# Eight feed-forward sublayers take the residual turned before its norm

## The reference

```python
def rmsnorm_2(x, w):
    xf = x.astype(jnp.float32)
    y = xf * lax.rsqrt(jnp.mean(xf * xf, axis=-1, keepdims=True) + NORM_EPS)
    return (y * w.astype(jnp.float32)).astype(x.dtype)

def swiglu_2(x, w_in, w_out):
    g, u = jnp.split(x @ w_in, 2, axis=-1)
    return (jax.nn.silu(g) * u) @ w_out

for i in range(DEPTH_2):
    h = h + 0.5 * rmsnorm_2(swiglu_2(rmsnorm_2(h, gn[0]), ffn1_w_in[i], ffn1_w_out[i]), gn[1])
    ... 
    h = h + 0.5 * rmsnorm_2(swiglu_2(rmsnorm_2(h, gn[4]), ffn2_w_in[i], ffn2_w_out[i]), gn[5])
```

## Time and profile before

| | us |
|---|---|
| Median of 3 runs | 2933.05 (2930.05 to 2938.34) |
| Profiled execution | 2926.79 |
| its span | 2925.0 |
| PE busy | 2684.2 (92%) |
| DVE busy | 1658.7 (57%) |
| ACT busy | 1293.4 (44%) |
| POOL busy | 195.2 (7%) |
| mean granted TensorE clock | 0.952 of full |

### The profile page before, as it was taken

The page is one execution under the profiler, slowest core; times in us unless marked ns, Lnnn a source line. Parts: engine busy times, 40 slices in busy tenths (PEclk is TensorE's granted clock), DMA queues, the critical chain, the costliest instruction groups (busy, mean ns, idle before and its releaser), DMA issues.

```text
span 2925.0 us, 45048 instructions
## 1 busy us (share of the span) xinstructions
PE 2684.2 (92%) x18537; PEld 2506.4 (86%) x18537; DVE 1658.7 (57%) x1846; ACT 1293.4 (44%) x1609; POOL 195.2 (7%) x323
## 2 busy tenths in 40 slices
PE   5879989799999888999999799999799999898898
PEld 4869988699899887998989699899789989898898
DVE  6667865564545665445456554554654454575544
ACT  3644346443434554444444443444443444464543
POOL 2210002000000211000000100000000000011000
PEclk9989999899999898999999899999899999999999
DMA  8639834475555333655554355465355545442453
GB/s 284 209 123 329 320 125 145 151 244 177 176 186 186 120 122 123 202 185 165 182 180 137 101 185 188 152 199 186 126 179 186 186 166 186 151 145 101 156 182 123
DMA packets 349162, 509.52 MB, mean 174 GB/s; under 512 B 9056, under 2 KB 302119, under 8 KB 344935
## 3 DMA queue, kind: packets, MB, share of 16 engines
q1 hardware_dynamic: 343216, 493.42, 50.3%
q0 software_dynamic: 3808, 11.66, 1.2%
q10 hardware_dynamic: 2006, 2.60, 0.3%
HBM read 505.80 MB, written 1.84 MB: 174 GB/s over the span
## 4 chain that ended last, share of the span: by engine, by line
PE 83%; DVE 6%; ACT 5%; issue 2%; POOL 2%; DMA 1%; DVEq 0%; ACTq 0%; POOLq 0%
PE B L514 18%; PE B L515 18%; PE B L516 18%; PE Y L514 8%; PE Y L516 8%; PE Y L515 8%; ACT w_hi L1207 2%; DVE tmp L1714 1%; DVE x L1717 1%; ACT junk L1218 1%; POOL stat L2389 1%; POOL stat L2392 1%; DVE w_lo L1686 1%; DVE h_lo L1745 1%; DMA raw<-in_w_ada 1%
## 5 line engine op out<-in xcount | busy, mean ns | idle before, releaser
L1686 DVE TENSOR_TENSOR w_lo<-raw,w_hi 128x2048 fp32r<-128x2048 f32 x425 | 966.0, 2276 | 564.8 <-ACT w_hi L1207 562.4
L1207 ACT ACTIVATE w_hi<-raw 128x2048 fp32r<-128x2048 f32 x425 | 805.0, 1899 | 590.1 <-PE B L516 541.8
L514 PE MATMUL B<-h_hi,w_hi 128*128 128x256 f32 x3712 | 1052.0, 283 | 8.9 <-DVE h_lo L1745 4.9
L515 PE MATMUL B<-h_lo,w_hi 128*128 128x256 f32 x3712 | 1048.5, 282 | 0.0
L516 PE MATMUL B<-h_hi,w_lo 128*128 128x256 f32 x3712 | 1048.0, 282 | 0.0
L514 PEld LDWEIGHTS B<-h_hi,w_hi 128*128 128x128 f32 x3712 | 705.3, 190 | 15.1 <-issue 11.7
L515 PEld LDWEIGHTS B<-h_lo,w_hi 128*128 128x128 f32 x3712 | 702.8, 189 | 4.1 <-issue 0.5
L516 PEld LDWEIGHTS B<-h_hi,w_lo 128*128 128x128 f32 x3712 | 704.3, 190 | 0.0
L514 PE MATMUL Y<-w_hi,a_hi 128*128 128x512 f32 x812 | 319.3, 393 | 0.9 <-DVE M L2193 0.5
L516 PE MATMUL Y<-w_hi,a_lo 128*128 128x512 f32 x812 | 318.6, 392 | 0.0
L515 PE MATMUL Y<-w_lo,a_hi 128*128 128x512 f32 x812 | 317.5, 391 | 0.0
(11 more groups left out here) (293 smaller groups left out, 2674.4 us busy)
## 6 DMA issues: line engine op xcount, KB each, us to landing
raw<-in_ffn_w_in SPq DMA_DIRECT2D x176, 1024.0 KB, 5.1
raw<-in_ffn_w_out SPq DMA_DIRECT2D x88, 1024.0 KB, 4.9
raw<-in_w_gate_up SPq DMA_DIRECT2D x44, 1024.0 KB, 5.2
raw<-in_hgrn_w_in SPq DMA_DIRECT2D x32, 1024.0 KB, 5.3
raw<-in_w_ada SPq DMA_DIRECT2D x24, 1024.0 KB, 5.2
M<-in_w_ada SPq DMA_DIRECT2D x24, 1024.0 KB, 8.0
raw<-in_w_down SPq DMA_DIRECT2D x22, 1024.0 KB, 5.0
raw<-in_w_in SPq DMA_DIRECT2D x14, 1024.0 KB, 5.5
```

Of the source, the lines that this page charges most:

```text
L514: pe.matmul(o, lh, rh, start=first, stop=False)
L515: pe.matmul(o, lh, rl, start=False, stop=False)
L1207: act.activation(w_hi[st.n % RING][:, 0:n], raw[st.r % RING][:, 0:n], ACT.Copy).then_inc(unit_rounded, 1)
L1686: dve.tensor_tensor(w_lo[s][:, 0:n], raw[st.r % RING][:, 0:n], w_hi[s][:, 0:n].bitcast(F32), ALU.subtract).then_inc(unit_split, st.step("" ...
```

## The change

It concerns the feed-forward sublayers `0a` to `3b` of the second stack, eight of them (`folded(p)`). At the boundary into one:

- PE transposes x itself, not xn. For tile 0 it does so inside the last product into Y of the sublayer before, ahead of that product's last three matmuls; for tile 1 in the middle of the first up product of tile 0.
- The squares of x move on ACT behind h_hi of each tile; POOL makes both tiles' inverse rms in one go, writes two diagonals of it (128x128), and epsilon times (mean square + epsilon) for the post norm. DVE's xn is gone.
- The first gate's silu takes the inverse rms as scale, in two halves of 256. Later gates, with tokens along the free axis, are multiplied by a row of the inverse rms on DVE (`scaled`), from PSUM to SBUF, and silu reads that. The row comes from two products of `ones` with the diagonals into B[3] and a copy by ACT. Up is not scaled; the missing factor goes out in the post norm, with the changed epsilon.
- PE's gate product waits for `scaled` instead of `silu`.

At the boundaries that are not folded, `lo(lead)` on DVE moves from before `pre(p, 0)` to after `pre(p, 1)`, ahead of `to_h(p, 1)`.

```diff
-            def into_y_tile(t, hi, lo, lh, ll, first, last):
+            def into_y_tile(t, hi, lo, lh, ll, first, last, follower=None):
                 for k in range(2):
                     for c in range(2):
+                        if follower and k == 1 and c == 1:
+                            turned_input(follower, 0)
...
+            def turned_input(p, t):
+                pe.wait_ge(vector_step, st.at(f"{input_of[p]}.x{t}"))
+                for k in range(KD):
+                    mm = pe.transpose(B[4 + 2 * t + k // 4][:, (k % 4) * P:(k % 4) * P + P], x[:, t, k * P:k * P + P], ident[:, :])
+                    if k % 4 == 3:
+                        mm.then_inc(tensor_step, st.step(f"{p}.tr{t}.{k // 4}"))
+            def first_pair_folded(p, works):
+                units = []
+                for i, (work, name) in enumerate(works):
+                    units.append(unit())
+                    if i == 0:
+                        work(*units[i], 0, p)
+                    else:
+                        work(*units[i], 0, None, lambda: turned_input(p, 1))
+                for i, (work, name) in enumerate(works):
+                    work(*units[i], 1, p if i == 0 else None)\
+                        .then_inc(unit_multiplied, st.step(name, unit_multiplied))
+                pe.wait_ge(gpsimd_step, st.at(f"{p}.diagonal"))
+                for t in range(NT):
+                    mm = pe.matmul(B[3][:, t * P:t * P + P], ones[:, :], inverse_diagonal[:, t * P:t * P + P], start=True, stop=True)
+                mm.then_inc(tensor_step, st.step(f"{p}.inverse"))
...
+                        if halfway and k == KD // 2:
+                            halfway()
...
+                    if folded(p):
+                        pe.wait_ge(vector_step, st.at(f"{p}.{prev}.scaled", back))
+                    else:
+                        pe.wait_ge(scalar_step, st.at(f"{p}.{prev}.silu", back))
...
+                if folded(p):
+                    act.wait_ge(st.sem_of(f"{post}.y0"), st.at(f"{post}.y0"))
+                    square(f"{post}.psq0", 4, Yt[:, 0, :])
+                    hi(lead)
+                    to_h(p, 0)
+                    act.wait_ge(st.sem_of(f"{post}.y1"), st.at(f"{post}.y1"))
+                    square(f"{post}.psq1", 5, Yt[:, 1, :])
+                    act.wait_ge(vector_step, st.at(f"{prev}0"))
+                    square(f"{p}.sq0", 0, x[:, 0, :])
+                    to_h(p, 1)
+                    act.wait_ge(vector_step, st.at(f"{prev}1"))
+                    square(f"{p}.sq1", 1, x[:, 1, :])
+                    return
...
+                    if folded(p) and before:
+                        act.wait_ge(vector_step, st.at(f"{p}.{tag}.scaled"))
+                        act.activation(tmp[:, 0:2 * S], gate_scaled, ACT.Silu).then_inc(scalar_step, st.step(f"{p}.{tag}.silu"))
+                    elif folded(p):
+                        act.wait_ge(gpsimd_step, st.at(f"{p}.rs"))
+                        for t in range(NT):
+                            mm = act.activation(tmp[:, t * S:t * S + S], B[0][:, t * S:t * S + S], ACT.Silu, scale=stat[:, 2, t:t + 1])
+                        mm.then_inc(scalar_step, st.step(f"{p}.{tag}.silu"))
+                    else:
+                        act.activation(tmp[:, 0:2 * S], B[0], ACT.Silu).then_inc(scalar_step, st.step(f"{p}.{tag}.silu"))
                     hi(KD * CH)
+                    if folded(p) and not before:
+                        act.wait_ge(tensor_step, st.at(f"{p}.inverse"))
+                        copy(inverse_row, B[3][:, 0:S]).then_inc(scalar_step, st.step(f"{p}.inverse.ev"))
...
+                post_norm(0)
+                if folded(p):
+                    lo(lead)
+                    to_h(p, 0)
+                    post_norm(1)
+                    to_h(p, 1)
+                    return
                 if p:
-                    if done:
-                        dve.wait_ge(vector_step, st.at(f"{done}.x1"))
+                    pre(p, 0)
+                post_norm(1)
+                if p:
+                    dve.wait_ge(vector_step, st.at(f"{done}.x1"))
                     to_h(p, 0)
                     pre(p, 1)
+                    lo(lead)
                     to_h(p, 1)
...
+                def scaled(tag):
+                    if folded(p):
+                        dve.wait_ge(unit_multiplied, st.at(f"{p}.{tag}.gate"))
+                        if tag == "second":
+                            dve.wait_ge(scalar_step, st.at(f"{p}.inverse.ev"))
+                        tt(shape3(gate_scaled, 2), shape3(B[0], 2), inverse_row.unsqueeze(1).to_broadcast([P, 2, S]), ALU.mult)\
+                            .then_inc(vector_step, st.step(f"{p}.{tag}.scaled"))
                 def body(tag, prev, before=True, c=0):
                     if before:
                         lo(2 * D)
+                        scaled(tag)
...
+            def folded_rms(post, t):
+                pool.wait_ge(scalar_step, st.at(f"{post}.psq{t}"))
+                i = 4 + t
+                pool.tensor_scalar(stat[:, 1, i:i + 1], stat[:, 0, i:i + 1], 1.0 / D, stat[:, 3, t:t + 1], ALU.mult, ALU.add)\
+                    .then_inc(gpsimd_step, st.step(f"{post}.prs{t}.ms"))
+                pool.wait_ge(gpsimd_step, st.at(f"{post}.prs{t}.ms"))
+                pool.tensor_tensor(stat[:, 2, i:i + 1], stat[:, 1, i:i + 1], half_power[:, 0:1], ALU.pow)\
+                    .then_inc(gpsimd_step, st.step(f"{post}.prs{t}"))
             def boundary(post, p):
                 for t in range(NT):
-                    if post:
+                    if folded(post):
+                        folded_rms(post, t)
+                    elif post:
                         rms(f"{post}.prs{t}", f"{post}.psq{t}", 4 + t, 5 + t, D)
-                    if p:
+                    if p and not folded(p):
                         rms(f"{p}.rs{t}", f"{p}.sq{t}", t, t + 1, D)
+                if folded(p):
+                    rms(f"{p}.rs", f"{p}.sq1", 0, 2, D)
+                    pool.wait_ge(gpsimd_step, st.at(f"{p}.rs"))
+                    for t in range(NT):
+                        d = pool.tensor_scalar(inverse_diagonal[:, t * P:t * P + P], ident[:, :], stat[:, 2, t:t + 1], 0.0, ALU.mult, ALU.add)
+                    d.then_inc(gpsimd_step, st.step(f"{p}.diagonal"))
+                    pool.tensor_scalar(stat[:, 3, 0:2], stat[:, 1, 0:2], EPS, 0.0, ALU.mult, ALU.add).then_inc(gpsimd_step, st.step(f"{p}.eps"))
+                    pool.wait_ge(gpsimd_step, st.at(f"{p}.eps"))
```

More of the change, by code:

```diff
@@ L358, in program, with folded @@
         names = [f"{i}{c}" for i in range(4) for c in "amb"]
+        input_of = dict(zip(names, ["F1"] + names))
+        next_of = {p: n for n, p in input_of.items()}
+        def folded(p):
+            return p is not None and p[0] not in "MF" and p[1] in "ab"
+        inverse_row = xn[:, 0, 0:S]
+        inverse_diagonal = xn[:, 1, 0:S]
+        gate_scaled = xn[:, 0, 2 * S:4 * S]
         def jobs_of(p):
@@ L573, in into_y_pair @@
                         before(t, i)
-                        mm = into_y_tile(t, *units[i], lh, ll, first and i == 0, last and i == 1)
+                        mm = into_y_tile(t, *units[i], lh, ll, first and i == 0, last and i == 1,
+                                         next_of.get(p) if last and t == 1 and i == 1 and folded(next_of.get(p)) else None)
                         if t:
@@ L660, in last_inputs @@
                         pe.wait_ge(vector_step, st.at(f"{p}.{(names[-1], 'last')[i]}.act"))
[L662 removed]
+                (first_pair_folded if folded(p) else first_pair)\
+                    (p, ((by_tokens(B[0], CH), f"{p}.first.gate"), (by_tokens(B[1], CH), f"{p}.first.up")))
                 pe.wait_ge(scalar_step, st.at(f"{p}.first.silu"))
@@ L1281, in ffn @@
                 act.wait_ge(unit_multiplied, st.at(f"{p}.last.gate"))
-                act.activation(tmp[:, 0:2 * S], B[0], ACT.Silu).then_inc(scalar_step, st.step(f"{p}.last.silu"))
+                if folded(p):
+                    act.wait_ge(vector_step, st.at(f"{p}.last.scaled"))
+                act.activation(tmp[:, 0:2 * S], gate_scaled if folded(p) else B[0], ACT.Silu).then_inc(scalar_step, st.step(f"{p}.last.silu"))
                 hi(2 * D)
@@ L1704, in boundary, with post_norm @@
             def boundary(done, p, n=0, factor=1.0, lead=0):
-                for t in range(NT):
-                    if done:
[L1710 to L1722, removed]
+                def post_norm(t):
+                    dve.wait_ge(gpsimd_step, st.at(f"{done}.prs{t}"))
+                    dve.wait_ge(st.sem_of(f"{done}.post"), st.at(f"{done}.post"))
+                    if t:
+                        dve.wait_ge(vector_step, st.at(f"{done}.x0"))
+                    dve.scalar_tensor_tensor(tmp[:, :], Yt[:, t, :], stat[:, 2, 4 + t:5 + t], post[n][:, :],
+                                             ALU.mult, ALU.mult)
+                    dve.drain()
```

(12 more changed lines are left out.)

7 lines of the change are left out of this document (3 added, 4 removed).

## The result

The changed kernel takes 2880.64 us (median of 4, 2877.24 to 2885.07); the kernel before, run beside it on the same chip, 2935.7 (median of 4, 2930.05 to 2939.88). The ratio is 0.9819, 95% interval 0.9804 to 0.9835: 55.1 us less. Forecast were 2899 and a range of 2884 to 2917: right in direction, 18 us short, and 3.4 us past the range's fast end.

What follows compares the result with a forecast made beforehand. PE was taken to bound the kernel, busy 92% of 2925.0 us, with gains only at sublayer boundaries. Boundary gain 43, less 7 for the clock and 2 for the moved w_lo, is 34 off the 2933.05 median: 2899, range 2884 to 2917.

Steps and rivals of the forecast that it cites:

- The schedule of a folded boundary: At the eight folded boundaries, S to DVE's first multiply falls from 27.44 to 22.0: 5.4 each, 43 in all.
- S: At each sublayer boundary, the start of ACT's square of the first token tile's Y; times are counted from it.
- The 0.4 that I added for semaphores: Allowance at each folded boundary for semaphores not counted, raising the worked-out 21.6 to 22.0.
- The clock: Gate of tile 0 after PE's 1.7 gap: half clock costs 1.7 at half of the eight boundaries, 7 in sum.
- of the rivals the first: Clock holds at all eight folded boundaries: 43 - 2 = 41 saved, 2892; chance 0.20.
- Rival 2: Clock lost at each of the eight folded boundaries, 2.3 each, 18 in sum: 23 saved, 2910; chance 0.18.
- The moved w_lo: At the seven other boundaries: nothing before a first pair, 0 to 0.9 lost at three before hgrn and pooling, 2 in sum.
- The row product: 80 DVE multiplies of gate chunks, 0.69 each, 55 in all, hidden under slack of 6.8: costed at nothing.
- Rival 4: Row product delays w_lo in every chunk beyond its 6.8 of slack; all 80 exposed cost 55: slower, 2954; chance 0.04.

Runs made afterwards that it cites:

- the kernel with 3.16: The changed kernel with two idle 128x512 adds on DVE between w_lo and first h_lo at the folded boundaries, PE's gap 3.16: 2909.23 us, ratio 0.9917.
- row_plus4: The changed kernel with four more row products, into a buffer nobody reads, ahead of each of the 80: 2909.02 us, ratio 0.9915.

## Why the prediction was right or wrong

**The schedule of a folded boundary** came as worked out: h_hi at S + 5.52 (forecast 5.44), first gate product at S + 8.22 (8.34), x of tile 1 at S + 12.53 (12.6), waiting for its h_lo 0.54 (0.6), w_hi of the second gate at S + 16.58 (16.6), w_lo with 0.94 to spare (0.7), first multiply at S + 21.6 in the mean (21.6 worked out, 22.0 used). The two products with ones pushed PE's next product from 1331.89 to 1332.25, 0.36 (0.3). The 0.4 that I added for semaphores wasn't there, but the sublayers give back 0.5 each behind the first multiply, the products with ones among it. So the mechanism was right, but that 43 meets the 42.7 of the profiles so closely is luck: over the eight, the 0.4 that I held back is 3 us in sum, what the sublayers give back is 4, and they nearly cancel.

**The clock**, priced at 7, cost nothing in the changed kernel. The gap was right (1.60 against 1.7), its price not. The first step that failed was "I price a loss below the old one ... and take it at half of the boundaries". In place of four losses the profiles show none: 0 of 8 fell, 1m to 1b included, which I had called likely. The 1.76 gap of the earlier trace rows that held the clock was the nearer neighbour, and of the rivals the first is the true case, as far as the clock goes; its 2892 is still 11 too high. The experiments show how near the other cases were: half a microsecond more, and the clock was gone at four to six of eight. Rival 2 (lost at each) describes the kernel with 3.16, though a loss cost 1.4 there and not 2.3.

The rule of the Trainium skill ("TensorE: Matmul & The Clock Gate", Part 4: PE-mode transpose), that transposes don't count as PE being busy like products, speaks for a fall here: without the transposes, only three products, some 0.7 us, lie between 1315.32, where they start, and the first gate product at 1318.72. The clock held at all eight. What the transposes count for isn't shown by that; only that the rule did not decide.

**The moved w_lo** had the wrong sign: a loss of 2 was forecast, and by itself it gained 6.7. The second step that failed is "Before a first pair ... PE does gate of tile 0 in between: nothing". I looked only at what w_lo would now delay, at its new place, and not at what it had delayed at its old one, although its price stood in the earlier trace rows and in my own text: POOL's 1.06, of which 0.87 was waiting. At each of the seven boundaries that POOL operation, xn and the transposes stand on the path that sets the first product. With the move by itself it comes 0.8 to 0.9 earlier at the four first pairs and 0.4, 0.8 and 0.4 at the whole_input ones, where 0.1 to 0.5 is paid back, where 0.7 was forecast. How 0.8 becomes 2.4 and 3.5 in the stretches of M1 and 1m isn't shown; the clock, which changes level several times in 1m, is likely a part. The Trainium skill's "SBUF — State Buffer", Terms, says that VectorE and GpSimd share a pair of ports which one of them holds for a full instruction; the trace agrees: POOL's operation ended 0.05 after w_lo (1515.29 and 1515.24).

**The row product** cost nothing, as forecast, but my reason was only half of one. I gave it 6.8 of slack from a loop turn; the place with the least slack is the last chunk, with 0.8, which I had not read. That is what is left beyond the one row product: by that, a second (0.7) would have fitted there, a third not, and the forecast would have called it free. Rival 4 had its mechanism in the wrong place. (The 0.8 is what row_plus4's 3.06 left over its wait of 2.28; runs with two or three row products weren't made.)

**The sum.** Forecast was 2933.05 - 34 = 2899; it is 18.4 too high. The clock makes 7.0 of that, the moved w_lo 7.3 (from a loss of 2 to the gain of 5.3 that the profiles show outside the eight sublayers, with whatever else differs there), the eight sublayers -0.3. For the last 4.4 no mechanism is shown: the profiled execution of before ran 6.3 below the median from which I subtracted, that of after 1.9 below its own, and stretches that no edit touches differ by as much. The range left room for the clock, but none for a gain at the seven other boundaries, and by that it missed.

## What to carry to other kernels

When an instruction is moved, cost the place it leaves as well as the place it takes: who ran beside it there, and was its neighbour slow? An operation of 128 numbers that takes a microsecond is the sign. When work is added to a repeated chunk, read its slack in the chunks at the ends, too: here only the second and the last ever made PE wait, never the loop turn that I had read. And a gap of the matrix engine has two prices, its length and what the clock does behind it; here none was paid behind gaps of 1.6 us, and behind gaps of 2.1, where it was paid, it was more than the half microsecond of delay that brought it.

## What the runs showed that I had not expected

- A POOL operation that meets DVE's w_lo (2.29, two SBUF inputs) waits for its end. In the changed kernel it happens to another one, harmlessly (timeline, 0b to 1a; w_lo ends at 1331.31):

```profile
1327.27 0.19 POOL L2475 TENSOR_SCALAR stat<-stat 128x2 f32<-128x2 f32 x1 [6.87 <-ACT junk L1264]
...
1328.35 0.72 POOL L2505 TENSOR_SCALAR xn<-ident,stat 128x128 f32<-128x128 f32 x2
1329.16 2.20 POOL L2507 TENSOR_SCALAR stat<-stat 128x2 f32<-128x2 f32 x1
```

  The two diagonals themselves took 0.72, some 0.36 each, and were as good as done when w_lo began (1329.07 against 1329.02).
- The clock behind gaps of nearly one length differs from boundary to boundary: 2.23 kept it and 2.07 lost it in one and the same kernel. With gaps of 2 to 3 us each loss cost 1.2 to 1.5 us of the first pair.
- Stretches that no edit touches (the start, 0m, 1m, 3m) differ by 2 to 5 us between kernels, and the start and 0m by 2.4 and 1.9 between the two profiles of the changed kernel alone. A difference of that size between two kernels is no mechanism until a place in the trace shows it.
